# Two chained transformer blocks in fp32: every SBUF tile behind the token matrix placed 128 bytes higher

## What is computed

```python
def first_block(x, ...):
    h = rms_norm(x, norm_gain)
    proj = einsum('bsd,dc->bsc', h, w_in)          # 1024 -> 10 x 1024 columns
    out_a = stick_breaking_attention(...) * silu(sb_g)      # 8 heads of 128
    out_b = rms_norm(chunkwise_retention(...)) * silu(r_g)  # 4 heads of 256
    p_a, p_b = out_a @ w_branch_sb, out_b @ w_branch_ret
    merged = sigmoid(m_sb + b0) * p_a + sigmoid(m_ret + b1) * p_b
    return x + merged @ w_out

def second_block(x, ...):
    h = concatenate([meta_tokens, x])              # 16 tokens in front
    u = rmsnorm(h); proj = u @ w_in_2
    h = h + concatenate([gla_mixer(...), swa_mixer(...)]) @ w_out_2
    h = h + square(relu(rmsnorm(h) @ w_ff1)) @ w_ff2
    return rmsnorm(h)[:, 16:]
```

## Time and profile before

| | |
|---|---|
| runs, us | 2437.97, 2439.99, 2440.59 (median 2439.99) |
| profiled execution: time / span from first to last instruction, us | 2438.28 / 2436.5 |
| mean granted TensorE clock | 0.998 of full speed |
| TensorE matmuls busy | 2404.9 us (99%), x12042 |
| TensorE weight loads busy | 1973.6 us (81%) |
| VectorE / ScalarE / GpSimd busy, us | 1613.6 / 1030.9 / 238.9 |
| DMA moved | 285.90 MB, mean 117 GB/s |

### The profile page before, as it was taken

The page is one execution under the profiler, slowest core; times in us unless marked ns, Lnnn a source line. Parts: engine busy times, 40 slices in busy tenths (PEclk is TensorE's granted clock), DMA queues, the critical chain, the costliest instruction groups (busy, mean ns, idle before and its releaser), DMA issues.

```text
span 2436.5 us, 30593 instructions
## 1 busy us (share of the span) xinstructions
PE 2404.9 (99%) x12042; PEld 1973.6 (81%) x12042; DVE 1613.6 (66%) x2079; ACT 1030.9 (42%) x1751; POOL 238.9 (10%) x395
## 2 busy tenths in 40 slices
PE   7999999999999999999999999999999999999998
PEld 6888888888887777889888877887888888888887
DVE  7777656556556766377742654267567776789889
ACT  6466422233335656123422346234545444533334
POOL 2011111111110000100010003000001211100000
PEclk9999999999999999999999999999999999999999
DMA  4322333333334231734232410100333444673433
GB/s 154 100 104 100 108 104 108 100 108 108 108 123 145 79 116 63 262 100 178 78 115 89 130 35 20 41 30 18 115 123 123 162 147 158 242 259 141 156 122 120
DMA packets 141775, 285.90 MB, mean 117 GB/s; under 512 B 18470, under 2 KB 91744, under 8 KB 134848
## 3 DMA queue, kind: packets, MB, share of 16 engines
q1 hardware_dynamic: 109168, 175.45, 21.7%
q0 software_dynamic: 32464, 108.49, 12.6%
HBM read 200.02 MB, written 83.89 MB: 117 GB/s over the span
## 4 chain that ended last, share of the span: by engine, by line
PE 90%; DVE 5%; DMA 2%; ACT 1%; DVEq 1%; issue 1%; ACTq 0%; SPq 0%; POOL 0%
PE ps L2785 38%; PE ps L621 13%; PE ps L3466 8%; PE ps L3049 7%; PE ps L2844 2%; PE ps L2863 2%; PE ps L615 2%; PE ps L3356 2%; PE ps L2891 2%; PE ps L2872 1%; PE ps L3341 1%; PE ps L2752 1%; PE ps L2964 1%; PE ps L2979 1%; PE ps L3034 1%
## 5 line engine op out<-in xcount | busy, mean ns | idle before, releaser
L1991 DVE TENSOR_TENSOR proj_out<-ps,proj_out 128x512 f32<-128x512 f32 x334 | 223.3, 685 | 248.9 <-PE ps L2785 234.9
L2785 PE MATMUL ps<-a_hi,pw_hi 128*128 128x512 f32 x600 | 235.2, 392 | 0.0
L2785 PE MATMUL ps<-a_lo,pw_hi 128*128 128x512 f32 x600 | 233.5, 389 | 0.0
L2785 PE MATMUL ps<-t_hi,pw_hi 128*128 128x512 f32 x560 | 219.3, 392 | 0.0
L2785 PE MATMUL ps<-t_lo,pw_hi 128*128 128x512 f32 x560 | 218.0, 389 | 0.0
L2785 PE MATMUL ps<-a_hi,pw_lo 128*128 128x512 f32 x400 | 155.9, 390 | 0.0
L2785 PEld LDWEIGHTS ps<-a_lo,pw_hi 128*128 128x128 f32 x600 | 112.7, 188 | 23.0
L2785 PEld LDWEIGHTS ps<-a_hi,pw_hi 128*128 128x128 f32 x600 | 112.6, 188 | 22.9
L1264 ACT ACTIVATE pw_hi<-pw_raw 128x512 fp32r<-128x512 f32 x150 | 83.6, 621 | 107.4 <-DMA pw_raw<-in_w_in 61.8
L1918 DVE TENSOR_TENSOR pw_lo<-pw_raw,pw_hi 128x512 fp32r<-128x512 f32 x200 | 128.4, 683 | 0.2
L2785 PEld LDWEIGHTS ps<-t_lo,pw_hi 128*128 128x128 f32 x560 | 105.2, 188 | 21.5
(11 more groups left out here) (531 smaller groups left out, 6190.4 us busy)
## 6 DMA issues: line engine op xcount, KB each, us to landing
pw_raw<-in_w_in SPq DMA_DIRECT2D x36, 1024.0 KB, 5.8
projections<-proj_out POOLq DMA_DIRECT2D x112, 256.0 KB, 3.5
hidden_raw<-hidden_forms SPq DMA_DIRECT2D x28, 1024.0 KB, 4.8
pw_raw<-in_w_ff SPq DMA_DIRECT2D x16, 1024.0 KB, 6.0
w_quarter<-in_w_ff SPq DMA_DIRECT2D x16, 1024.0 KB, 6.8
hidden_forms<-proj_out POOLq DMA_DIRECT2D x56, 256.0 KB, 3.1
hidden_forms<-nb POOLq DMA_DIRECT2D x56, 256.0 KB, 3.4
w_raw<-in_w_in SPq DMA_DIRECT2D x10, 1024.0 KB, 5.2
```

The costliest lines, as they stand in the source:

```text
L1991: return dve.tensor_tensor(out_ap(n, j), product_bank(n, o), src, ALU.add)
L2785: last = pe.matmul(product_bank(n, o), w, a[:, k0 + k, t], start=(k == 0 and g == 0), stop=(k == 3 and g == 2))
```

## The change

One line advances the cursor by 128 bytes after `a_meta` is placed. Everything placed from the cursor later, and everything placed from `w_at`, `out_at`, `work_at` and `region`, starts 128 bytes higher; nothing before it moves. After it `w_at` is 92,928, `out_at` 125,696, `work_at` 158,464, and the highest tile ends at 229,120. No instruction, operand shape, wait or queue is added, removed or reordered.

```diff
@@ -89,6 +89,7 @@
     meta_at = cur[0]
     AM = at("a_meta", [P, KT, 2 * META], f32r)
     AM_hi, AM_lo = AM[:, :, 0:META], AM[:, :, META:2 * META]
+    cur[0] += 128
     w_at = cur[0]
     W_hi = [at(f"w_hi{s}", [P, KT, BC], f32r) for s in range(2)]
     raw_at = [cur[0], cur[0] + KT * BC * 4]
```

## The result

| | before | after |
|---|---|---|
| median of runs, us | 2438.86 (2437.29 to 2440.59) | 2458.37 (2457.74 to 2459.09) |
| ratio, 95% interval | | 1.0079 (1.0067 to 1.009) |
| span of the profiled execution, us | 2436.5 | 2456.5 |
| matmuls busy, us | 2404.9 | 2426.5 |

A forecast was written before the change was run, and what follows sets the result against it. The prediction took TensorE issuing its 12,042 matmuls as the bound (busy 2404.9 of 2436.5 us). Its terms, 0 + 0 + 0 + 0, left the forecast at the median, 2440.0 us, range 2435.5 to 2445.0, with 79% for no effect.

The forecast's parts named there:

- What bounds the kernel, and the two ways to be hit: TensorE's 12,042 matmuls bound the kernel; the change could alter their pace or cause delays that break other engines' and queues' cover.
- Matmuls on one side of the cut, cost 0: Matmuls with both operands before or both behind the 128-byte shift keep their distance, so their pace stays: 0 us.
- Matmuls across the cut, taken as 0: 4,440 matmuls with one operand in the token matrix, one behind it: between 59 us gain and 22 us loss, taken as 0.
- The second: Rival: the 4,440 pairs lose being in step and slow by 5.0 ns each, 22 us, to 2462 us; chance 5%.
- The first rival: In-step operands cost the fixed 13.3 ns on 4,440 matmuls; losing it gives 2381 us, 59 us faster; chance 5%.
- a possible gain of 45 us: Estimate if operand distance caused the trace's 11 ns above the page's gap on 4,056 matmuls of 512 columns.
- VectorE and ScalarE, 0: VectorE instructions might go from 683 to 693 ns, 1.5%, but TensorE would hide it: cost 0.
- DMAs, 0: Five chain pieces, 44.5 us: loss bound 4.4 us, gain bound 0.6 us from where transfers start in SBUF; taken as 0.
- the 6%: Stores from proj_out would start on a multiple of 256: 68 against 64 beats a row, 6% off, an estimated 0.3 us.

The follow-up runs named there:

- the run with everything up: Kernel before with the whole layout, ident and token matrix included, 128 bytes higher, so no distance between tiles changes: 2437.78 us, ratio 0.9997.
- the run with the keys up: Kernel before with stick-breaking attention's keys and work tiles behind them 128 bytes higher, out of step with the queries, in plain fp32: 2438.83 us, ratio 1.0001.
- with 96 bytes: Kernel before with the cursor advanced by 96 bytes in place of 128 behind the token matrix: 2466.45 us, ratio 1.0115.
- the run with 192 bytes: Kernel before with the cursor advanced by 192 bytes in place of 128 behind the token matrix: 2452.75 us, ratio 1.0059.
- with 64 bytes: Kernel before with the cursor advanced by 64 bytes in place of 128 behind the token matrix: 2458.60 us, ratio 1.0084.

## Why the prediction was wrong

**What bounds the kernel, and the two ways to be hit**: right. TensorE's waits did not change; only its pace did, and of 21.6 us more of busy time 20.0 reached the span.

**Matmuls on one side of the cut, cost 0**: right. 226.7 ns a step for the branch products in both. That their start addresses don't matter was shown by the run with everything up. The sum tiles, also on one side, took 2.0 us more, behind slowed products.

**Matmuls across the cut, taken as 0**: this is the step that failed. It chose between a gain of 59 us and a loss of 22 by what it took as the nearest rows, the 128x128 matmuls of aa and gv, which are out of step by 128 bytes and have the pace of retention's. That observation was true and did not carry over: they are plain fp32, and the run with the keys up shows that plain fp32 does not slow at 512 columns either. What the runs showed in its place: 232.4 ns a step instead of 226.7 for the output products, and 21.6 us more of matmul time in all. The prediction had said that the argument was "not airtight" for fp32r and still gave it 79%. The rows held no fp32r pair that is out of step at all, since by the layout every such pair starts in step, those of the earlier trace rows too; for that form the trace of before was silent, and silence should have left both ends of the bound with real weight. The count was a little short as well: 240 more matmuls of 512 columns cross the cut (96 of L2752, 96 of L621 with feed-forward weights, 48 of L3233 and L3245).

**The rivals.** The second was the truth. Its price, 5.0 ns a step on 4,440 matmuls from the steps behind a turn, 22 us, was close: measured 5.7 on the output products, and 19.5 us in all, since the 384 matmuls of 256 columns did not slow at all and the 408 gate products took only 0.5 us more. That the price fitted is luck as far as the runs go: no run tests whether the steps behind a turn are slow for the same reason (the last section has what speaks for it). What was held against it, that 231.7 occurs only behind turns with both sorts of pairs, was no evidence, as no pair out of step existed to be seen. The first rival had the same place with the opposite sign, and the measured pace refutes it for 512 columns: in step is the best of the eight distances tried.

The Trainium skill, "TensorE: Matmul & The Clock Gate", section "Step-by-step: what each phase is for", says that TensorE has two independent read ports in SBUF, so that loading the next weights takes no read bandwidth from the running matmul. The runs agree with it for plain fp32. For fp32r they speak against it: a step is 2.2 to 6.6 ns longer when the two operands are out of step, though which of them holds up the other is not shown.

The trace stood 11 ns above the gap given by the Trainium skill, "TensorE: Matmul & The Clock Gate", section "Back-to-back issue gap", and the prediction made a possible gain of 45 us out of them. The operands' distance is not their cause: no distance tried brought 512 columns under 226.7.

**VectorE and ScalarE, 0**: right (683 and 693 as before, busy within 0.5 us).

**DMAs, 0**: right. The chain of after has no DMA piece left of the two that lay at 2137 to 2161 us. That is not the work of a slower TensorE: they are gone from the chain with everything up as well, at the old pace, and are there with 96 bytes, the slowest run (9.56 and 15.42 us). Landings of stores from proj_out, which now start on a multiple of 256, against those from nb, which don't:

```profile
projections<-proj_out POOLq DMA_DIRECT2D x112, 256.0 KB, 3.4
...
hidden_forms<-proj_out POOLq DMA_DIRECT2D x56, 256.0 KB, 3.0
hidden_forms<-nb POOLq DMA_DIRECT2D x56, 256.0 KB, 3.4
```

3.5 and 3.1 became 3.4 and 3.0, and nb's 3.4 stayed. That has the direction of the 6% that the prediction had worked out from the Trainium skill, "DMA: Bandwidth & Descriptors", section "How a descriptor splits into AXI transactions", but it doesn't hold as evidence: with the tiles behind the matrix up by 256, where no alignment changed, the same three are 3.3, 3.5 and 3.4.

## What to carry to other kernels

Keep the weights and the moving operand of fp32r matmuls at the same place within 256 bytes: in this kernel being out of step costs 1% to 3% of a 512-column matmul and up to 1.15% of the whole time, and it is set by nothing but a tile's offset, so an odd-sized tile put in front of others can bring it in. When a profile shows the same matmul at two paces with no wait between them, compare where the operands start, and look for a turn or an interruption just before the slower ones. And when the trace has no example of the thing that a change makes, a neighbour of another data type is weak ground for "no effect".

## What the runs showed that was not expected

- The pace of 512-column fp32r matmuls depends on the start of the moving operand less that of the weights, modulo 256 bytes: 226.7 ns at 0; 228.9 at 64; 232.4 at 128; 233.3 at 32, 96, 192 and 224.
- A pair in step can be slow for a while. In the kernel before, a single 16x16 matmul at 1421.23 us interrupts a stretch of 512-column pairs, all in step. The first line below is the second pair behind it:

```profile
1421.73 0.40 PE L621 MATMUL ps<-a_lo,w_hi 128*128 128x512 f32 x1
...
1424.04 0.39 PE L621 MATMUL ps<-a_hi,w_lo 128*128 128x512 f32 x1
...
1426.76 0.39 PE L621 MATMUL ps<-a_hi,w_lo 128*128 128x512 f32 x1
```

From there ten steps take 2.31 us, 231.0 ns each, much as behind the turn of the earlier trace rows; the next twelve take 2.72, 226.7 each. Out of step, 216 output products in a row stay at 232.4. And in the run with 192 bytes, sum tiles in step that follow matrix products out of step rise, this group from 389 ns:

```profile
L2786 PE MATMUL ps<-ft_hi,ps_lo 128*128 128x512 f32 x120 | 47.2, 393 | 0.0
```

So the rows fit a pace that a disturbance raises, and that comes down to 226.7 again, within some ten steps, only when the operands are in step. No run was made to test this reading.
- For 256 columns being out of step never costs. The stretch of 192 such matmuls, in which w moves and the token matrix holds the weights, in the kernels before, after and with 64 bytes:

```profile
1584.51 23.04 PE ps L615 x192
```

```profile
1596.82 22.79 PE ps L616 x192
```

```profile
1597.75 21.76 PE ps L616 x192
```

120.0 ns a step in step, 118.7 out of step by 128, 113.3 out of step by 64. With 32, 96, 192 and 224 bytes the same stretch takes 22.40, 23.04, 21.76 and 22.72 us. So being in step is not free of cost either: in step a matmul takes 13.3 ns more than its columns' time at both sizes, while out of step it takes less than that at 256 columns (at 96 bytes as much) and more at 512. Why is open: the runs show that the distance between the starts of the two operands decides, and its period; they show neither how the two reads meet nor what repeats every 256 bytes. On the 384 matmuls of 256 columns 6.7 ns each would be 2.6 us, 0.1%, an estimate, if only they were put out of step by 64; that was not tried.
